# An expert layer whose down projection uses seven block products in place of eight

## The reference

```
def ec_moe(h, p):
    ...
    aff = jax.nn.softmax((xt @ p["w_router"]).astype(F32), axis=-1)
    cap = (EC_CAPACITY_FACTOR * T) // N_EXPERTS
    vals, idx = lax.top_k(aff.T, cap)
    xs = xt[idx]
    hid = jax.nn.silu(jnp.einsum("ecd,edf->ecf", xs, p["w_e_gate"])) * jnp.einsum("ecd,edf->ecf", xs, p["w_e_up"])
    ye = jnp.einsum("ecf,efd->ecd", hid, p["w_e_down"]) * vals[..., None].astype(h.dtype)
    y = jnp.zeros((T, D), h.dtype).at[idx.reshape(-1)].add(ye.reshape(-1, D))
```

## Time and profile before

| | |
|---|---|
| median of 3 runs | 3276.99 us (3272.01 to 3277.89) |
| profiled execution | 3273.48 us |
| its span, first to last instruction | 3271.6 us |
| mean granted TensorE clock | 0.967 |
| PE busy | 3085.6 us, 94% |
| DVE busy | 1911.9 us, 58% |
| ACT busy | 1413.3 us, 43% |
| POOL busy | 526.9 us, 16% |
| DMA | 630.73 MB, mean 193 GB/s |

### The profile page before, as it was taken

The page is one execution under the profiler, slowest core; times in us unless marked ns, Lnnn a source line. Parts: engine busy times, 40 slices in busy tenths (PEclk is TensorE's granted clock), DMA queues, the critical chain, the costliest instruction groups (busy, mean ns, idle before and its releaser), DMA issues. The chain is left out here.

```text
span 3271.6 us, 52938 instructions
## 1 busy us (share of the span) xinstructions
PE 3085.6 (94%) x20253; PEld 2673.1 (82%) x20253; DVE 1911.9 (58%) x3135; ACT 1413.3 (43%) x2101; POOL 526.9 (16%) x440
## 2 busy tenths in 40 slices
PE   7899999899979879999999984999999999999997
PEld 2378888798945779999997764999999999899996
DVE  5544443433345578776755558666666666666656
ACT  4633333422244145564644541444444444444446
POOL 1011111000023334101000003121111111112212
PEclk9999999999989889999999996999999999999998
DMA  8733332421199976767656443565655555565668
GB/s 329 264 113 114 126 106 90 153 60 60 57 313 361 362 241 219 232 218 229 216 171 202 155 149 131 197 204 193 199 195 192 193 185 183 183 208 195 198 205 311
DMA packets 334757, 630.73 MB, mean 193 GB/s; under 512 B 28408, under 2 KB 209912, under 8 KB 329865
## 3 DMA queue, kind: packets, MB, share of 16 engines
q1 hardware_dynamic: 308575, 568.47, 50.7%
q0 software_dynamic: 16992, 54.88, 5.6%
q10 hardware_dynamic: 8976, 4.46, 0.5%
HBM read 490.16 MB, written 137.56 MB: 192 GB/s over the span
## 5 line engine op out<-in xcount | busy, mean ns | idle before, releaser
L71 PE MATMUL experts_bank<-experts_xT_high,experts_w_high_gu 128*128 128x272 f32 x2048 | 596.2, 291 | 6.4 <-DVE experts_w_low_gu L3375 3.9
L73 PE MATMUL experts_bank<-experts_xT_high,experts_w_low_gu 128*128 128x272 f32 x2048 | 591.4, 289 | 0.0
L72 PE MATMUL experts_bank<-experts_xT_low,experts_w_high_gu 128*128 128x272 f32 x2048 | 589.6, 288 | 0.0
L71 PEld LDWEIGHTS experts_bank<-experts_xT_high,experts_w_high_gu 128*128 128x128 f32 x2048 | 386.1, 189 | 12.8 <-ACT experts_act_g L3198 5.3
L72 PEld LDWEIGHTS experts_bank<-experts_xT_low,experts_w_high_gu 128*128 128x128 f32 x2048 | 387.1, 189 | 4.6
L73 PEld LDWEIGHTS experts_bank<-experts_xT_high,experts_w_low_gu 128*128 128x128 f32 x2048 | 386.0, 188 | 0.0
L3375 DVE TENSOR_TENSOR experts_w_low_gu<-experts_w_raw_gu,experts_w_high_gu 128x1024 fp32r<-128x1024 f32 x256 | 302.6, 1219 | 25.3 <-ACT experts_w_high_gu L3151 20.5
L2146 PE MATMUL merge_bank<-merge_rows_high,merge_w_gates_high 128*128 128x272 f32 x896 | 261.4, 292 | 9.1 <-DVE merge_rows_low L2303 5.9
L3151 ACT ACTIVATE experts_w_high_gu<-experts_w_raw_gu 128x1024 fp32r<-128x1024 f32 x256 | 256.8, 1045 | 14.0 <-DMA experts_w_raw_gu<-in_w_stream 14.0
L2148 PE MATMUL merge_bank<-merge_rows_high,merge_w_gates_low 128*128 128x272 f32 x896 | 260.6, 291 | 0.0
L2147 PE MATMUL merge_bank<-merge_rows_low,merge_w_gates_high 128*128 128x272 f32 x896 | 259.2, 289 | 0.0
(11 more groups left out here) (435 smaller groups left out, 7256.4 us busy)
## 6 DMA issues: line engine op xcount, KB each, us to landing
experts_w_raw_gu<-in_w_stream SPq DMA_DIRECT2D x256, 512.0 KB, 4.6
experts_w_raw_d<-in_w_stream SPq DMA_DIRECT2D x128, 512.0 KB, 6.7
merge_rows_b<-scratch_hT SPq DMA_DIRECT2D x52, 544.0 KB, 5.4
filters_wm<-in_w_mod SPq DMA_DIRECT2D x12, 2048.0 KB, 11.2
merge_rows_t<-scratch_row_sums SPq DMA_DIRECT2D x36, 544.0 KB, 6.7
merge_y<-scratch_yhy SPq DMA_DIRECT2D x32, 544.0 KB, 5.1
merge_y<-scratch_yret SPq DMA_DIRECT2D x32, 544.0 KB, 4.7
x_early<-in_xT SPq DMA_DIRECT2D x17, 512.0 KB, 5.2
```

The lines of the kernel that those rows point to most:

```text
L71: pe.matmul(out, lhs[0], rhs[0], start=start, stop=False)
L72: pe.matmul(out, lhs[0], rhs[1], start=False, stop=False)
L73: return pe.matmul(out, lhs[1], rhs[0], start=False, stop=stop)
```

## The change

**Block products.** For experts 0 to 13 the down projection of 256 latent tokens (hidden 256x1024 times weights 1024x1024) is taken as a product of 2x2 blocks (128x512 times 512x512) with seven block products (Winograd's form of Strassen's scheme). Each is 4 x 3 matmuls of 512. Experts 14 and 15 keep the eight row steps.

**Right operands.** With b11 to b22 the blocks of the weights: t1 = b12 - b11 and t3 = b22 - b12 are made by VectorE over 128x2048 (`block_sum`). For t2 = b22 - t1 and t4 = b21 - t2 in their own buffers, ScalarE writes the negated t1 (or t2) over a block (`negated`, 128x2048) and POOL issues a transfer that adds a block from memory to it (`block_sum` of POOL, `accum_op`, 1 MB). The seven operands are split in 14 parts of 128x1024 each, in a ring of 3 (before: 8 blocks, ring of 4).

**Left operands.** Hidden rows 0 to 3 keep their product of gate and up; ScalarE and VectorE split only the first 128 tokens of it. With rows 4 to 7 VectorE makes four more sums of 128x128 (each waits for an earlier one but the first), and ScalarE and VectorE then split six blocks at once (128x768). No weight split stands between the product and the low part any more.

**Order.** The seven products of expert e run during expert e+1, behind columns 0, 1, 3, 5, 6, 8 and 9 (`BEHIND`); products 3 to 6 go into banks whose contents are reused: ScalarE copies bank 0 after products 0, 3 and 4 (`copied`), the next product is accumulated on top, and VectorE evicts with an addition and a scaling (`summed`, 128x512 each) or a scaling (`gated`). Splits are laid to columns by hand (`SPLIT_AT`, `SPLIT_NEXT`), the lead of gate/up splits is three blocks instead of two, and the masks of the expert after next stand at columns 1, 3, 5, 6 and 8 (`PASSED_AT`). SP loads the eight down blocks in two groups of four at columns 9 and 10. The counting matmuls come before the context product, not after. Context rows are scaled by VectorE in four pieces straight from `pcx`, then by ScalarE. POOL scatters expert e-1 during expert e, behind the next gather and the two adding transfers. In expert 14 both the products of 13 and the row steps of 14 run. The last expert's output tiles are handled in batches of 5, 5, 4 and 3 at fixed columns, with 11 instead of 13 buffers.

The core of the diff:

```
-STREAM = ["g0", "u0"] + sum([[f"g{f}", f"u{f}", f"d{f - 1}"] for f in range(1, KT)], []) + [f"d{KT - 1}"]
+STREAM = [f"{n}{f}" for f in range(KT) for n in "gu"]
...
-LEAD = 2
-RINGS = {"gu": 4, "d": 4}
+LEAD, RING, RING_D = 3, 4, 3
...
+OPERANDS = ["b11", "b21", "t1", "t2", "t3", "t4", "b22"]
+PARTS = [f"{name}{i}" for name in OPERANDS for i in range(2)]
+BEHIND = {0: 0, 1: 1, 3: 2, 5: 3, 6: 4, 8: 5, 9: 6}
+SPLIT_AT = {1: [3, 4], 2: [5], 4: [6, 7], 5: [8], 6: [9], 8: [10, 11], 9: [12, 13]}
+SPLIT_NEXT = {13: 0, 14: 1, 15: 2}
+D_FIRST = (1, 6, 8, 9)
+LATE = NE - 2
...
+        ROWS_AT = {9: (0, 1, 2, 3), 10: (4, 5, 6, 7)}
+        PASSED_AT = {1: (0, 2), 3: (2, 5), 5: (5, 7), 6: (7, 13), 8: (13, NLAT)}
```

On TensorE:

```
+                def block_product(e, j):
+                    to = pd[:, (0, 1, 2, 0, 0, 0, 2)[j], :]
...
+                    elif j < 6:
+                        pe.wait_ge(AY.sem, AY.at(e, ("p1", "u2", "u3")[j - 3]))
...
+                        pe.wait_ge(VP.sem, VP.at(e, PARTS[n]))
+                        for q in (2 * i, 2 * i + 1):
...
                 def body(e, h, k, one, two):
...
+                        if 0 < e <= LATE and i in BEHIND:
+                            block_product(e - 1, BEHIND[i])
```

In ScalarE's body:

```
+                    for i in range(NS):
+                        f = i // 2
+                        products = 0 < e <= LATE
+                        if products and i == 2:
+                            copied(e - 1, 0, "p1")
+                        if products and i == 6:
+                            copied(e - 1, 3, "u2")
+                        if products and i == 7:
+                            copied(e - 1, 4, "u3")
+                        for todo in splits(e, i):
+                            split(*todo)
+                        if products and i == 1:
+                            negated(e - 1, "t2")
+                        if products and i == 4:
+                            negated(e - 1, "t4")
+                        if i % 2 == 0:
...
+                            act.activation(act_g[:], pg[:, 0:SLOTS], ACT.Silu).then_inc(*AG.inc(f"g{f}"))
...
+                                act.wait_ge(VG.sem, VG.at(e, f"w{f}"))
+                                act.wait_ge(DP.sem, DP.at(e - 1, "b221"))
+                                act.activation(hh[:, f - HALF, 1:7, :], sums[:], ACT.Copy).then_inc(*AH.inc(f"h{f}"))
```

On VectorE, the hidden rows 4 to 7 and the body:

```
+                def hidden(e, f):
...
+                    v.tensor_tensor(sums[:, 3, :], full[:, q, 0, :], full[:, q, 1, :], ALU.subtract).then_inc(*VG.inc(f"x{f}"))
+                    done("m")
+                    v.tensor_tensor(sums[:, 1, :], full[:, q, 1, :], sums[:, 4, :], ALU.add).then_inc(*VG.inc(f"z{f}"))
+                    done("z")
+                    v.tensor_tensor(sums[:, 2, :], sums[:, 1, :], full[:, q, 0, :], ALU.subtract).then_inc(*VG.inc(f"y{f}"))
+                    done("y")
+                    v.tensor_tensor(sums[:, 5, :], sums[:, 0, :], sums[:, 2, :], ALU.subtract).then_inc(*VG.inc(f"w{f}"))
...
+                    for i in range(NS):
+                        f = i // 2
+                        products = 0 < e <= LATE
+                        if products and i == 0:
+                            block_sum(e - 1, "t1")
+                        for todo in splits(e, i):
+                            split(*todo)
+                        if products and i == 3:
+                            block_sum(e - 1, "t3")
+                        if products:
+                            evicted(e - 1, i)
...
+                        if i % 2:
+                            hidden(e, f)
...
+                            low(e, f)
```

In POOL's body, behind the gather:

```
+                    if 0 < e <= LATE:
+                        for name in ("t2", "t4"):
+                            block_sum(e - 1, name)
+                        scatter(e - 1)
```

More of the change, by code:

```diff
@@ L3033, in index @@
                                 pe.wait_ge(dve_below, n + 1)
[L3034 removed]
+                            pe.matmul(pi[:, half:half + 1], (tally if e else below)[:, n, P * half:P * half + P], ones[:],
                                       start=(n == 0), stop=(n == tiles - 1))
@@ new lines, in low @@
+                def low(e, f):
+                    steps = VE if e >= LATE else VG
+                    v.wait_ge(AH.sem, AH.at(e, f"h{f}"))
+                    hid_done(v, e, f"m{f}" if e >= LATE or f < HALF else f"w{f}")
+                    if e >= LATE:
+                        to, src, high = hid(f)[1], full[:, f % HALF], hid(f)[0]
+                    elif f < HALF:
+                        to, src, high = hl[:, f, 0, :], full[:, f, 0, :], hh[:, f, 0, :]
+                    else:
+                        to, src, high = hl[:, f - HALF, 1:7, :], sums[:], hh[:, f - HALF, 1:7, :]
+                    v.tensor_tensor(to, src, high.bitcast(F32), ALU.subtract).then_inc(*steps.inc(f"l{f}"))
@@ L3453, in body @@
                                 v.wait_ge(PI.sem, PI.at(e + 1, "ids"))
-                            for n in range(3 * part, min(3 * part + 3, NLAT)):
+                            for n in range(*PASSED_AT[part]):
                                 passed(e + 2, n)
-                            if part == 5:
+                            if part == 8:
                                 passed_context(e + 2)
-                        if one and f == KT // 2:
+                        if one and i == KT:
@@ new lines, in body @@
+                    v.wait_ge(CP.sem, CP.at(e - 1, "added"))
+                    if final(e):
+                        v.wait_ge(yst[4], 32)
+                    for c in range(4):
+                        rows = slice(32 * c, 32 * c + CCAP)
+                        v.tensor_tensor(ye[0:CCAP, 2, CUT * c:CUT * c + CUT], pcx[rows, 0:CUT], gate2c[rows, :], ALU.mult)\
+                         .then_inc(*VC.inc(f"k{c}"))
+                    if final(e):
+                        scaled(*BATCHES[3])
@@ L3570, in store_final, with block_sum @@
                     g.dma_start(tile_out(t), spots[SPOT[t]]).then_inc(yst[SPOT[t]], 16)
-                def finish(h):
-                    for t in range(10):
+                def block_sum(e, name):
+                    low, right = ADDEND[name]
+                    at = e * NR + NS + HALF * low
+                    g.wait_ge(AN.sem, AN.at(e, name))
+                    g.dma_start(quarter(name), d["w_stream"][at:at + HALF, :, 512 * right:512 * right + 512].rearrange("f p c -> p f c"),
+                                accum_op=ALU.add).then_inc(added[name], 16)
```

650 lines of the change are left out of this document (411 added, 239 removed).

## The result

The changed kernel takes 3391.51 us (median of four, 3387.61 to 3391.92) against 3276.57 us (3272.01 to 3277.89) of the kernel before on the same chip: ratio 1.0349, 95% interval 1.0336 to 1.0362. The forecast was 3316 us with a range up to 3350: the direction was right, the loss three times as large as forecast, +115 instead of +39. The profiled execution has a span of 3389.6 us, 118.0 more than before.

What follows compares the result with a forecast made beforehand. VectorE's and ScalarE's hand-overs were taken to bound middle experts at 79.3 us. -20 + 13 x (79.3 - 76.26) + 20.7 + 0 + 1.3 = +41.5 us on a profiled 3273.48 gave 3316 us, range 3256 to 3350.

Steps and rivals of the forecast that it cites:

- TensorE saves 2.80 us per expert: Down projection: seven block products replace eight row steps, one step of 2.80 us less for each of 14 experts, 39.2 us.
- VectorE's work, 67.1 us: Middle experts 1 to 13: VectorE's instructions sum to 67.1 us per expert, against 47.97 before.
- Waits inside the hidden row, 5.1: Rows 0 to 7: VectorE stands for ScalarE's conversion, 0.35 us each in rows 0 to 3, 0.9 in rows 4 to 7.
- for each other's order, 7.1: Columns 2 to 8 of a middle expert: VectorE waits for ScalarE's in-order work, together 7.1 us, making the loop 79.3 us.
- The 0.9 us behind TensorE at column 3: Column 3 of a middle expert: VectorE waits 0.9 us for the SiLU behind TensorE's column 2.
- They cost nothing: SyncE's eight row loads at columns 9 and 10: wanted some 10 us later, landing in 4.6 to 6.7 us, so no cost.
- The adding transfers at zero: POOL's two 1 MB adds per expert: first lands at A + 19, wanted at A + 19.2; zero, bounds 0 to 5 us.
- A: Time mark in a middle expert: the end of VectorE's context copies, from which the prediction followed one expert.
- the rival of late adds: Adding transfers land late: 3 us more on each of 13 experts, 3355 us; needs landings of 13.5 us or more; chance 0.10.
- Expert 0, -20: Expert 0 has no down work: 58 us instead of 78, -20.
- Expert 14, +20.7: Expert 14 carries seven products and eight row steps: 95.9 us, with some waits 97, +20.7.
- the fourth rival: TensorE's granted clock falls after its wait before the counting matmul: 1.7 us in each of 13 experts, 3338 us; chance 0.15.

Runs made afterwards that it cites:

- e11: Changed kernel with even columns' splits moved between hidden product and low part, row loads in twos behind columns 8 to 11, sums t2 and t4 on VectorE: 3253.2 us.
- e16: e11 with the final norm spread over eight columns of the last expert and its down rows split later: 3247.4 us, ratio 0.9914.
- e2: Changed kernel without the matmuls of the high part with the low part of the weights in the seven block products: 3390.5 us.
- e15: Changed kernel with sums t2 and t4 on VectorE and row loads in twos behind columns 8 to 11, splits in the changed kernel's order: 3377.1 us.
- e5: Changed kernel without the two adding transfers of an expert, negations kept: 3359.2 us.
- e13: Changed kernel with the row loads two by two behind columns 8 to 11, nothing else: 3356.1 us.
- e1: Changed kernel with the eight row loads issued in pairs at columns 9, 10, 11 and 12: 3353.7 us.
- e14: Changed kernel with sums t2 and t4 as subtractions on VectorE instead of negations and adding transfers: 3410.2 us.
- e7: Changed kernel with the last expert's final norm issued one or two tiles behind each of eight columns instead of in batches: 3383.9 us.
- e10: e9 with sums t2 and t4 formed by subtractions on GpSimd instead of negations and adding transfers: 3316.6 us.
- e9: Changed kernel with even columns' splits moved between hidden product and low part, and row loads in twos behind columns 8 to 11: 3287.3 us.

## Why the prediction was right or wrong

**TensorE saves 2.80 us per expert.** Right, and it can be had: 73.3 us in e11 and e16. In the changed kernel it is not the bound (e2).

**VectorE's work, 67.1 us.** Right: 67.66.

**Waits inside the hidden row, 5.1, and for each other's order, 7.1.** Right as a mechanism, and the moved splits take most of both away (e15 to e11). In size the first is 4.8 us. Of the second, the five hand-overs behind a copy, a conversion or the negation (columns 2, 4, 5, 6 and 8) were put at 5.75 us and measure 1.14, 0.66, 1.44, 1.14 and 0.66, together 5.0, in the expert of e5 that starts near 2736 us, where there are no adding transfers of weights. The 0.9 us behind TensorE at column 3 shows in some experts only. That e13 gives 12.2 us in all, as forecast, is partly luck: late transfers fill what is missing.

**"They cost nothing" of SyncE's row loads.** This is the first failed step. I compared the time until the rows themselves are wanted with landings of 4.6 to 6.7 us, medians of loads that were spread evenly, and asked only whether the rows would delay the context. The victim is the gate/up block queued behind them, 14.60 us to its landing. It costs 2.4 us of period (e1; 2.5 in e13) and some 5.5 us of expert 14, 38 and 35 us of the time.

**The adding transfers at zero: "no cost, and none to spare".** The second failed step. The landing was near, median 10.1 us for 10.5 taken, but the first transfer of an expert takes 11.1 in the median and up to 12.4, and in experts 1 to 13 it is issued 9.1 to 9.3 us after A instead of 8.3. So it lands 19.0 to 21.7 us after A, and ScalarE, which was to want it at 19.2, waits for it in nine of 14 experts. That is the rival of late adds, with a smaller price than its 3 us per expert, 1.9 us of period and 32 us of the time (e5). That rival's condition was misread: the 4.9 to 15.9 us are of a view that also counts loads from `xacc`; the adding scatters alone took 9.3 to 11.3 us, so they gave no case for 13.5 us, and none was needed. The negations were worth what their term said.

These terms are not a sum to be added to 41.5: in the order of removal, e13 and e14 show that each gain depends on the others, and e1 also shortens the waits for adding transfers, from 18.6 to 5.6 us. No run takes out the burst and the transfers together and leaves the negations and the order of the splits as they are.

**Expert 0, -20.** By the places of the result section this is -14.6: up to the context product the step's own numbers give 58 - 3.8 = 54.2 against 68.8, and the other 5.6 us are the two row steps behind it. It was -12.3, with a start 4.7 us later that I can't explain; that start lies between 2027.4 and 2035.7 us in the other runs, whose edits come behind it.

**Expert 14, +20.7.** Too low, though 20.7 and 22.1 look alike. The 97 us end behind two row steps that follow the context product; by the same places as the measured +22.1 they are 91.4, +15.1. The burst and the adding transfers are in the missing 7.0 us too: 98.4 us fall to 92.9 without the burst (e1) and to 94.0 without the adding transfers (e5). In e11 this expert takes 89.6.

**Expert 15, "waits of like size, 0 +- 4", and the end, +1.3.** The third failed step: +22.3. A batch of five tiles holds ScalarE for 12 us between a hidden row's conversion and the next splits, where the kernel before had two or three tiles at a time. e7 returns 10.4 us of it. What the other 12 are wasn't taken apart; VectorE still waits 7.8 us once for a conversion there.

**Clock.** 0.97 to 0.98 in the middle experts: a part of the fourth rival is there. The granted clock falls to 0.50, the lower of its two levels (1.2 and 2.4 GHz), 13 times in experts 1 to 13, for instance at 2338.63, just behind a wait of TensorE of 2.35 us. What it cost was not priced apart.

By places, the forecast is -14.6 + 39.5 + 15.1 + 1.3 = +41.3, and the span came out 76.7 us above it: 41.7 in experts 1 to 13 (3.2 each), 21.0 from the context product of expert 14 on, 7.0 in expert 14, 4.7 by the late start and 2.3 in expert 0.

## What to carry to other kernels

When a change gathers transfers into a burst, price the burst on what is queued behind it, and not by the median landing of the transfers when they were spread. Its own size over the rate would have come near here: eight blocks of 512 KB at the 318 GB/s of that stretch are 13 us (an estimate, made afterwards), and the block behind them took 14.6. And a transfer that is forecast to land just as it is wanted has a price: here a landing up to 3 us later made ScalarE wait in nine of 14 experts. When one engine's work rises to within some per cent of the bound, its order against the engine that feeds it decides: here moving splits into the gap between a product and its low part was worth 124 us with no instruction saved, and nearly 5 us more work on the fuller engine cost nothing once it was done. The saving on TensorE was there from the start; it took three edits (order, row loads, sums) before the time showed it, and each of them alone, and each pair that was run, left the kernel slower than before.

## What the hardware showed

GpSimd's subtraction of 128x2048 took 4.61 us in one place and 6.80 in another, and single instructions of VectorE beside it took far longer than their own time. GpSimd's timeline in e10, and VectorE's:

```profile
2491.06 4.61 POOL L3833 TENSOR_TENSOR experts_w_raw_d<-experts_w_raw_d 128x2048 f32<-128x2048 f32 x1 [2.47 <-DVE experts_w_low_d L3541]
2504.10 6.80 POOL L3833 TENSOR_TENSOR experts_w_raw_d<-experts_w_raw_d 128x2048 f32<-128x2048 f32 x1 [8.44 <-DVE experts_w_low_d L3541]
```

```profile
2493.17 3.58 DVE L3532 TENSOR_TENSOR experts_w_low_gu<-experts_w_raw_gu,experts_w_high_gu 128x1024 fp32r<-128x1024 f32 x1 [2.06 <-ACT experts_w_high_gu L3258]
...
2505.22 1.21 DVE L3541 TENSOR_TENSOR experts_w_low_d<-experts_w_raw_d,experts_w_high_d 128x1024 fp32r<-128x1024 f32 x1
2506.36 0.68 DVE L3549 TENSOR_TENSOR experts_ye<-experts_bank,experts_ye 128x512 f32<-128x512 f32 x1
2507.07 4.38 DVE L3556 SCALAR_TENSOR_TENSOR experts_ye<-experts_ye,experts_vals,experts_gate 128x512 f32<-128x512 f32 x1
```

The split that starts at 2493.17, with GpSimd already at work, ends 1.08 us after GpSimd's end (2495.67), so it did its 1.21 us of work then. At 2504.10 VectorE was first: its splits run at their own 1.21 us until 2506.43, and GpSimd's 6.80 us are 2.3 of standing and 4.5 of work. The add from a bank in PSUM at 2506.36 takes its own 0.68 us beside GpSimd; the scaling at 2507.07, which reads two SBUF tiles, ends 0.55 us after GpSimd does, for 0.75 of work. That is 6.0 us of VectorE's time in this expert, in the engine that had none to spare; over experts 2 to 13 its busy time is 72.8 us each, against 66.7 in e9 with the same instructions on it. The Trainium skill's page "SBUF — State Buffer", section "Who interferes with whom", says that a VectorE instruction with two SBUF inputs and a GpSimd instruction that reads SBUF block each other, and that the one that comes first keeps the other out for its whole length; these rows agree, both ways round.

The 1 MB adding transfers landed in 10.1 us in the median. The estimate in the prediction from the Trainium skill's page "DMA: Bandwidth & Descriptors", section "Anatomy of one DMA — SWDGE (gpsimd) path", was 4.4 us; the measurement decides, and the rows of adding scatters were the better guide. Issued behind the gather, the first of the two lands so late that ScalarE waits for it in nine experts of the changed kernel, and 4.0 to 6.1 us in every expert of e9.
